# Pre-norm deferred past the input projections of a two-layer encoder trunk

## The chip, the cores and the metric

The kernel runs on one core of a Trainium2 chip. The metric is the device time of one execution in microseconds (us); less is better. The core has five engines that run side by side: PE (TensorE, matrix products and transposes), ACT (ScalarE), DVE (VectorE), POOL (GpSimd) and SP (SyncE, which here only issues DMAs). They meet at semaphores.

## The reference, cut to what matters

Two layers over x (256 tokens, 1024 features). Each layer:

```python
h = _rmsnorm(x, pre_norm_g[i])                 # x / rms(x) * g
z = h @ w_in[i]                                # 1024 -> nine column groups
qa, ka, va, qi, ki, wi, ga, qb, kb, vb, gb = _split_in(z)
# rotary embedding on qa, ka, qi, ki, qb, kb; wi * IDX_HEADS ** -0.5
oa = _dsa_attention(qa, ka, va, qi, ki, wi, top_k)    # indexer picks 64 keys, softmax over these
ob = _diff_attention(qb, kb, vb, lam, lam_init, subln_g[i])
y = concat([oa * silu(ga), ob * silu(gb)]) @ w_out[i]
x = x + _rmsnorm(y, post_norm_g[i])
e = (p[i] @ w_ple_proj[i]) * sigmoid(x @ w_ple_gate[i])
x = x + _rmsnorm(e, ple_norm_g[i])
```

All is float32. p is (2, 1, 256, 256): one embedding input of 256 features for each layer.

## The kernel before

**Tiles.** The tokens are two blocks b of 128 rows. x lives in `resid`. Weights come in units: each is two slices of 128 input rows by 512 columns (512 KB); the indexer's units, `IDX`, have 324 columns (324 KB). `UNITS` (L48) lists them in the order of use: `PLE` (the product with p, one unit for each half n of the output), nine groups of `w_in` (`IDX`, `QB`, `KB`, `VB`, `QA`, `KA`, `VA`, `GB`, `GA`) of four units each, then `WO` and `WG`. SP loads a unit into one of 5 slots of `raw`, and waits first for `lo_done`, that the unit five earlier has been split (L400).

**Split products.** float32 operands are split in two parts, as `w_hi` + `w_lo` (ACT copies, L522; DVE subtracts, L708), and each product is made of three: hi·hi (L951), hi·lo (L952), lo·hi (L953). The activations are transposed by PE (step `t8`, L993: four 128x128 transposes to a half of 512 columns in a PSUM bank `sc`), and are split in the same way (`act_hi` L522, `act_lo` L744).

**Steps.** All engines walk through one list, `layer_steps`, each taking its share of each step. ACT and DVE also carry the units' splits, put in by `all_steps` (`START` by hand for the first ten, the rest some seven or eight pieces ahead of use). A piece `mm` is one unit for one block b, that is six products. The list fixes the order on each engine, so a step that waits on ACT holds back what stands behind it on ACT.

**The pre-norm.** Step `pre` for block b: ACT squares and sums the rows of `resid` (L527), DVE adds eps (L701), POOL takes the power -0.5 (L470), DVE multiplies `resid` by that and by `g_norm`, the weight copied to all partitions (L739, into `work`). Only then can `t8` of h begin (L975), and after it the first `IDX` piece. The weights come by a broadcast load of 512 KB for each layer (L407, L512).

**Around it at the start.** SP issues p, PLE unit 0, x of block 0, PLE unit 1, the pre-norm weight, x of block 1, and the first IDX unit. PE runs warm-up products, transposes p, runs warm-up products again (L970), then the four PLE pieces with the transposes of h between them. POOL issues, after h is made, the next layer's p (L433), the post-norm weight (L506), four small broadcast loads of the lambda vectors (L437) and one of `subln_g` (L438), and the weight `g_ple` (L509).

**At the border of the layers** the last WG pieces of layer 0 are followed by PLE pieces with the transposes of h for block 0, then `IDX` and `QB` for block 0, and the same for block 1.

**Banks.** Four PSUM banks `proj` take the products in turn (`bank_of`, L317; `wait_bank`, L889). ACT evicts them, with plain copies for most groups, sigmoid for the gates.

Of the kernel before, what the change touches and what calls it, by code (L numbers as in the profile page):

```python
# [22 lines left out]
P = 128  # L23
# [24 lines left out]
UNITS = [("PLE", n, 0, KU, N) for n in range(2)]  # L48
# [10 lines left out]
for _i, _u in enumerate(UNITS):  # L59
# [7 lines left out]
START = [1, 2, 5, 8, 11, 11, 16, 17, 18, 19]  # L67
HOLD = 2
# [6 lines left out]
    TI=0,  # L75
    D=3,
    lam=4,
    QB=[4, 5],
    KB=[10, 13],
    QA=[25, 30],  # L80
    KA=[33, 38],
    S=[12, 16, 19, 36, 41, 43],
    E=[12, 18, 23, 37, 41, 44],
    R=[16, 16, 19, 22, 24, 24, 38, 41, 43, 44, 44, 44],
    PT=[19, 23, 26, 41, 42, 44, 46, 49, 50],
    PV=[20, 25, 28, 42, 44, 46, 49, 51, 51],
    hv=[21, 28],
    hn=[23, 30],
    topk=[[0, 0, 1, 4, 6, 6, 8, 12], [12, 24, 24, 26, 26, 27, 31, 31]],
    y=[51, 54])  # L90


def layer_steps(L):
# [26 lines left out]
    ple = [(n, b) for n in range(2) for b in range(NB)]  # L120
    t8 = lambda src, b: [("t8", src, b, 0), ("t8", src, b, 1)]
    y8 = lambda b, half: [("t8", "y", b, half)]
    if L == 0:
        out += [("pT", 0), ("pre", 0, 0)]
        mms("PLE", ple, {0: [("pre", 1, 0)], 2: t8("h", 0), 3: t8("h", 1)})
        mms("IDX", both, {})
        mms("QB", both, {3: [("TI", 0)], 5: [("D", 0)]})
    else:
        out += [("ple0", 1, 1, L - 1)]
        mms("PLE", ple, {0: t8("h", 0) + [("psq", 1, 1, L - 1), ("ple1", 1, L - 1)], 2: [("pre", 1, L)]})  # L130
        mms("IDX", one(0), {})
        mms("QB", one(0), {1: t8("h", 1)})
        mms("IDX", one(1), {})
        mms("QB", one(1), {1: [("TI", 0)], 3: [("D", 0)]})

    mid = [[] for _ in range(7 * len(both))]
    placed = [(PLACE["TI"], ("TI", 1)), (PLACE["D"], ("D", 1)), (PLACE["lam"], ("lam",))]
    for kind in ("S", "E", "R", "PT", "PV"):
        placed += [(i, (kind, n)) for n, i in enumerate(PLACE[kind])]
    for kind in ("hv", "hn"):  # L140
        placed += [(i, (kind, b)) for b, i in enumerate(PLACE[kind])]
# [9 lines left out]
    for c, chunk in enumerate(["KB", "VB", "QA", "KA", "VA", "GB"]):  # L151
        mms(chunk, both, dict(enumerate(mid[c * len(both):(c + 1) * len(both)])))
    mms("GA", one(0) + one(1), dict(enumerate(mid[6 * len(both):])))
# [7 lines left out]
                      12: ([("pre", 0, L + 1)] if L + 1 < DEPTH else []) + [("psq", 1, 0, L)]})  # L161
# [5 lines left out]
def all_steps():  # L167
# [9 lines left out]
    for i, pos in enumerate(pieces):  # L177
# [3 lines left out]
        if L and u < 2 and i - first_use[L * U] < HOLD:  # L181
            held.add(i)
# [5 lines left out]
    at = 0  # L188
# [15 lines left out]
def build(nc, x, p, pre_norm_g, w_in, w_out, post_norm_g, lambda_q1, lambda_k1, lambda_q2, lambda_k2, subln_g,  # L204
# [6 lines left out]
    with ctx:  # L211
# [40 lines left out]
        g_norm = sb("g_norm", [P, D_MODEL])  # L252
        g_ple = sb("g_ple", [P, D_MODEL])
# [35 lines left out]
        x_in = [sem(f"x_in{b}") for b in range(NB)]  # L289
        p_in = [sem(f"p_in{L}") for L in range(DEPTH)]  # L290
        gpre_in = [sem(f"gpre_in{L}") for L in range(DEPTH)]
# [5 lines left out]
        h_done, x1_done, x2_done = sem("h_done"), sem("x1_done"), sem("x2_done")  # L297
# [19 lines left out]
        def bank_of(chunk, n, b):  # L317

            if chunk == "PLE":
                return 2 * (1 - n) + b  # L320
            if chunk in ("WO", "WG"):
                return (2 if b == 0 else 0) + n
            return 2 * (IN_CHUNKS.index(chunk) % 2) + b
# [59 lines left out]
        def _(sp):  # L383
            def load_x(b):
                sp.dma_start(resid[:, b, :], x[0, b * P:(b + 1) * P, :]).then_inc(x_in[b], 16)

            sp.dma_start(p_raw[:, :, :], p[0, 0].rearrange("(b p) d -> p b d", p=P)).then_inc(p_in[0], 16)
            for g in range(DEPTH * U):
                L, u = divmod(g, U)
                chunk, n, k0, nk, cols = UNITS[u]  # L390
                if chunk == "PLE":
                    src = w_ple_proj[L, :, n * N:(n + 1) * N]
# [495 lines left out]
        def _(pe):  # L888
# [39 lines left out]
            for pos, (L, s) in enumerate(STEPS):  # L928
                kind = s[0]
                if kind == "mm":  # L930
# [25 lines left out]
                    elif last_k:  # L956
                        last.then_inc(b0_done, 1)
# [167 lines left out]
```

## Time and profile before

| | |
|---|---|
| median of three runs | 375.98 us (375.42 to 376.27) |
| profiled execution, its own time | 376.63 us |
| its span, first to last instruction | 374.8 us |
| PE busy | 362.0 us (97%) |
| DVE busy | 261.2 us (70%) |
| ACT busy | 223.0 us (59%) |
| POOL busy | 66.7 us (18%) |
| moved from HBM | 60.2 MB |

The busy share of PE counts products from start to modelled end, and they overlap; whether PE is held up is read from the starts of its rows in the timeline. In the timeline a row is an instruction or a run of like ones (x8), with its start, its time, and in brackets what the engine had waited for before it.

### The profile page before, as it was taken

Reading aid. Unit: us, or ns where it says so; the run is one execution under the profiler, and the core shown is the slowest. Engines: PE = TensorE matmul, PEld = TensorE weight load, DVE = VectorE, ACT = ScalarE, POOL = GpSimd, SP = SyncE. Lnnn points to the kernel's source line nnn. Section 1 sums busy time; section 2 is a strip of 40 time slices with the busy share of each in tenths; the row PEclk is TensorE's granted clock in tenths of the full one; section 3 lists DMA queues with packets and bytes.
Section 4 is the critical chain, followed back from the end, with each engine's and each line's share of the span. In section 5 each row is a group of like instructions: output and inputs, shape, how many; then the busy total and the mean of one; then the engine's idle time right before and its main releaser. Section 6 shows DMA issues by size and latency. Waiting matters only on the chain.

```text
span 374.8 us, 5604 instructions
## 1 busy us (share of the span) xinstructions
PE 362.0 (97%) x1932; PEld 300.6 (80%) x1932; DVE 261.2 (70%) x450; ACT 223.0 (59%) x451; POOL 66.7 (18%) x122
## 2 busy tenths in 40 slices
PE   7798999999999999999999999999999999999992
PEld 7596788788877888888889878788887788888881
DVE  2654977889873676587697478788986467558643
ACT  4655674775875753554684548577586575366221
POOL 1514513032500000004005512104150000000000
PEclk9899999999999999999999999999999999999999
DMA  7998846465564354567754845546457335551011
GB/s 251 319 183 312 290 141 186 114 174 162 165 194 149 113 170 143 184 201 146 201 164 150 267 126 157 168 120 207 124 168 226 112 114 168 171 176 47 2 41 71
DMA packets 32075, 61.64 MB, mean 164 GB/s; under 512 B 2384, under 2 KB 4688, under 8 KB 32048
## 3 DMA queue, kind: packets, MB, share of 16 engines
q1 hardware_dynamic: 30928, 58.01, 49.8%
q0 software_dynamic: 1120, 3.28, 4.6%
q8 instruction: 16, 0.26, 0.3%
q14 instruction: 11, 0.09, 0.1%
HBM read 60.23 MB, written 1.05 MB: 163 GB/s over the span
## 4 chain that ended last, share of the span: by engine, by line
PE 88%; DMA 6%; issue 2%; DVE 2%; ACT 1%; SPq 0%; DVEq 0%; POOLq 0%; POOL 0%
PE proj L951 25%; PE proj L953 24%; PE proj L952 23%; PE pv L1091 4%; DMA raw<-in_w_in_dram 3%; PE sc L1063 3%; PE sc L993 3%; DMA g_norm<-in_pre_norm_g_dram 2%; PE tr L1076 2%; PE tr L1009 2%; PE sc L1047 1%; PE sc L1023 1%; DVE w_lo L708 1%; DVE work L739 0%; ACT w_hi L522 0%
## 5 line engine op out<-in xcount | busy, mean ns | idle before, releaser
L951 PE MATMUL proj<-w_hi,act_hi 128*128 128x512 f32 (+1 forms) x416 | 166.4, 400 | 1.3 <-DVE w_lo L708 1.1
L953 PE MATMUL proj<-w_hi,act_lo 128*128 128x512 f32 (+1 forms) x416 | 160.1, 385 | 0.0
L952 PE MATMUL proj<-w_lo,act_hi 128*128 128x512 f32 (+1 forms) x416 | 159.9, 384 | 0.0
L708 DVE TENSOR_TENSOR w_lo<-raw,w_hi 128x1024 fp32r<-128x1024 f32 (+1 forms) x108 | 128.0, 1203 | 17.7 <-ACT w_hi L522 16.9
L522 ACT ACTIVATE w_hi<-raw 128x1024 fp32r<-128x1024 f32 (+1 forms) x108 | 109.9, 1041 | 6.9 <-DMA raw<-in_w_in_dram 4.9
L951 PEld LDWEIGHTS proj<-w_hi,act_hi 128*128 128x128 f32 x416 | 78.2, 188 | 17.3 <-DVE w_lo L708 1.3
L953 PEld LDWEIGHTS proj<-w_hi,act_lo 128*128 128x128 f32 x416 | 78.1, 188 | 16.0
L952 PEld LDWEIGHTS proj<-w_lo,act_hi 128*128 128x128 f32 x416 | 78.3, 188 | 12.8
L470 POOL TENSOR_TENSOR rstd<-var,minus_half 128x1 f32<-128x1 f32 x12 | 6.7, 554 | 192.2 <-DVE var L698 177.0
L625 ACT ACTIVATE probs<-sc,neg_max 128x128 f32<-128x128 f32 (+1 forms) x64 | 26.0, 429 | 13.4 <-DVE neg_max L796 13.4
L522 ACT ACTIVATE act_hi<-sc 128x512 fp32r<-128x512 f32 x24 | 13.6, 597 | 32.7 <-PE sc L993 32.7
L796 DVE TENSOR_REDUCE neg_max<-sc 128x2 f32<-128x512 f32 (+1 forms) x24 | 15.5, 686 | 17.5 <-PE sc L1063 17.5
L744 DVE TENSOR_TENSOR act_lo<-sc,act_hi 128x512 fp32r<-128x512 f32 x24 | 15.9, 686 | 15.2 <-ACT act_hi L522 15.0
L522 ACT ACTIVATE pT<-tr 128x512 f32<-128x512 f32 (+1 forms) x22 | 12.7, 578 | 22.3 <-PE tr L1076 20.3
L1091 PEld LDWEIGHTS pv<-v_all,pT 128*128 128x128 f32 x144 | 18.5, 191 | 1.3
L1091 PE MATMUL pv<-v_all,pT 128*128 128x64 f32 (+1 forms) x144 | 18.1, 271 | 0.0
L460 POOL TENSOR_TENSOR v_all<-work,rot_tab 128x128 f32<-128x128 f32 x16 | 12.1, 756 | 32.4 <-ACT work L522 31.4
L492 POOL TENSOR_TENSOR rstd_h<-var_h,minus_half 128x4 f32<-128x4 f32 x4 | 4.1, 1032 | 58.0 <-DVE var_h L838 58.0
L625 ACT ACTIVATION_READ_ACCUMULATOR probs<-sc,neg_max 128x1 f32 x64 | 13.8, 215 | 0.0
L522 ACT ACTIVATE work<-proj 128x512 f32<-128x512 f32 x16 | 9.6, 597 | 5.5 <-PE proj L953 5.5
L872 DVE TENSOR_TENSOR work<-work,emb 128x512 f32<-128x512 f32 x8 | 5.5, 686 | 10.2 <-ACT work L658 10.2
L785 DVE MAX8 top<-score 128x8 f32<-128x128 f32 (+1 forms) x32 | 11.4, 356 | 0.6
(124 smaller groups left out, 368.6 us busy)
## 6 DMA issues: line engine op xcount, KB each, us to landing
raw<-in_w_in_dram SPq DMA_DIRECT2D x64, 512.0 KB, 4.1
raw<-in_w_out_dram SPq DMA_DIRECT2D x16, 512.0 KB, 3.4
raw<-in_w_ple_gate_dram SPq DMA_DIRECT2D x16, 512.0 KB, 4.1
raw<-in_w_in_dram SPq DMA_DIRECT2D x8, 324.0 KB, 7.2
raw<-in_w_ple_proj_dram SPq DMA_DIRECT2D x4, 512.0 KB, 3.4
resid<-in_x_dram SPq DMA_DIRECT2D x2, 512.0 KB, 7.5
g_norm<-in_post_norm_g_dram POOLq DMA_DIRECT2D x2, 512.0 KB, 5.6
g_ple<-in_ple_norm_g_dram POOLq DMA_DIRECT2D x2, 512.0 KB, 7.5
```

Source lines behind the costliest of these rows:

```text
L460: nc.gpsimd.tensor_tensor(rot_a[:, 0:heads, :], view[:, :, 0:ROT], table(cos2, slice(0, ROT)), ALU.mult)
L522: return nc.scalar.activation(dst, src, ACT.Copy, scale=scale)
L625: last = nc.scalar.activation(probs[:, i % 4, j * keys:(j + 1) * keys], sc[i % 2][:, j * keys:(j + 1) * keys], ACT.Exp, bias=neg_max[:, i ...
L708: nc.vector.tensor_tensor(w_lo[:, g % SLOTS, 0:nk * cols], raw[:, g % RAW_SLOTS, 0:nk * cols], w_hi[:, g % SLOTS, 0:nk * cols].bitcast(fp3 ...
L744: nc.vector.tensor_tensor(act_lo[:, s[2], 4 * s[3]:4 * s[3] + 4, :].rearrange("p k t -> p (k t)"), sc[i % 2][:, :], act_hi[:, s[2], 4 * s[ ...
L785: link(nc.vector.max(top8[:, :], score[b][:, :]))
L796: nc.vector.tensor_reduce(neg_max[:, i % 2, 0:len(maps)], sc[i % 2][:, :].rearrange("p (m k) -> p m k", k=keys), AX.X, ALU.max, negate=Tru ...
L951: nc.tensor.matmul(ps, src_hi[:, b, k0 + k, :], hi, start=(first_u and k == 0), stop=False)
L952: nc.tensor.matmul(ps, src_hi[:, b, k0 + k, :], lo, start=False, stop=False)
L953: last = nc.tensor.matmul(ps, src_lo[:, b, k0 + k, :], hi, start=False, stop=last_k)
L993: last = nc.tensor.transpose(sc[i % 2][:, j * P:(j + 1) * P], tile, ident[:, :])
L1091: last = nc.tensor.matmul(pv[:, h * width:(h + 1) * width], pT[:, n % 3, j, :], v_all[:, kt, g, h * width:(h + 1) * width], start=(kt == 0 ...
```

## The change

It has five parts.

1. The pre-norm is taken apart. `t8` of h now transposes x itself, as soon as it is there (block and half by themselves). The weight of the pre-norm, which after the transpose lies along partitions, is applied on eviction: ACT copies four 128x128 pieces with a scale from a column of `g_col`, DVE subtracts with the same scale. 1/rms of a token is applied to the projections: on each ACT eviction (scale by `rstd`), and for the gates in the sigmoid's scale and in DVE's product. The factor `IDX_HEADS ** -0.5` moves into the relu's scale. The multiplication of `resid` into `work` is gone.
2. `g_col` is made once: a load of 8 KB with the weights of both layers, one transpose on PE (step `gT`), one copy on ACT. The two broadcast loads of 512 KB are gone.
3. PLE units are one slice each (256 KB, three products a piece), four in place of two. x comes in four loads of 256 KB, behind the PLE units.
4. The order: in both layers eight PLE pieces, then `IDX` for block 0, `IDX` for block 1, then `QB` and the rest. `pre` (the sum of squares) stands behind the transposes. `PLACE` and `START` are rewritten for it.
5. `bank_of` depends on the layer, and IDX takes the banks of PLE half 0. The small loads, and the next layer's p, are issued right after p is transposed; the post-norm weight and `g_ple` of layer 0 only at the third PV step.

```diff
-UNITS = [("PLE", n, 0, KU, N) for n in range(2)]
+UNITS = [("PLE", n, k, 1, N) for n in range(2) for k in range(D_PLE // P)]
...
-START = [1, 2, 5, 8, 11, 11, 16, 17, 18, 19]
-HOLD = 2
...
+    h00=[5, 5],
+    h01=[8, 8],
+    pre0=[9, 11],
+    psq=1,
+    ple1=3,
+    h10=[0, 3],
+    h11=[8, 10],
+    pre1=[10, 12],
+    HOLD=0,
+    START=[1, 1, 3, 3, 8, 11, 12, 12, 17, 18])
...
     if L == 0:
-        out += [("pT", 0), ("pre", 0, 0)]
-        mms("PLE", ple, {0: [("pre", 1, 0)], 2: t8("h", 0), 3: t8("h", 1)})
-        mms("IDX", both, {})
-        mms("QB", both, {3: [("TI", 0)], 5: [("D", 0)]})
+        out += [("pT", 0), ("gT",)]
+        side = []
...
+    side += [(i, ("t8", "h", b, half)) for b in range(NB) for half, i in enumerate(PLACE[f"h{L}{b}"])]
+    side += [(i, ("pre", b, L)) for b, i in enumerate(PLACE[f"pre{L}"])]
+    head = ple + [(len(ple) // NB + u, b) for u, b in one(0) + one(1)]
+    mms("PLE", head, {i: [step for at, step in side if at == i] for i in range(len(head))})
...
+                bank = 2 * ((IN_CHUNKS.index(chunk) + 1) % 2) + b
+            return bank ^ 2 * (L % 2)
...
                 if g == 0:
-                    load_x(0)
-                elif g == 1:
-                    sp.dma_start(g_norm[:, :], pre_norm_g[0, :].partition_broadcast(P)).then_inc(gpre_in[0], 16)
-                    load_x(1)
-                elif g == 2:
+                    sp.dma_start(g_rows[:, :], pre_norm_g.rearrange("l (k p) -> (l k) p", p=P)).then_inc(gpre_in, 16)
+                elif g == 3:
+                    load_x(0, 0)
+                    load_x(0, 1)
+                elif g == 4:
+                    load_x(1, 0)
+                    load_x(1, 1)
+                elif g == 5:
...
-                if kind == "t8" and s[1:] == ("h", 1, 1):
-                    pool.wait_ge(h_done, L * 2 + 2)
+                if kind == "pT" and s[1] + 1 < DEPTH:
+                    pool.wait_ge(ptr_done, s[1] + 1)
+                    load_p(s[1] + 1)
+                if kind == "pT" and s[1] == 0:
+                    load_small(0)
+                if kind == "PV" and s[1] == 2:
+                    if L > 0:
+                        pool.wait_ge(wo_scaled, L * 4)
                     pool.dma_start(g_norm[:, :], bcast(post_norm_g[L, :])).then_inc(gpost_in, 16)
                     if L == 0:
-                        load_small(0)
                         pool.dma_start(g_ple[:, :], bcast(ple_norm_g[0, :])).then_inc(gple_in, 16)
...
-                        copy(z_idx[:, b, 0:nqk], ps[:, 0:nqk])
+                        act.wait_ge(rstd_done[0], L * 2 + b + 1)
+                        copy(z_idx[:, b, 0:nqk], ps[:, 0:nqk], rstd[:, 0, b:b + 1])
...
-                        copy(z_view(chunk, b), ps[:, :]).then_inc(z_out, 1)
+                        copy(z_view(chunk, b), ps[:, :], rstd[:, 0, b:b + 1]).then_inc(z_out, 1)
...
+                    if s[1] == "h":
+                        act.wait_ge(gcol_done, 1)
+                        for j in range(4):
+                            k = 4 * s[3] + j
+                            last = copy(act_hi[:, s[2], k, :], sc[i % 2][:, j * P:(j + 1) * P],
+                                        g_col[:, L * KT + k:L * KT + k + 1])
+                        last.then_inc(at_hi, 1)
+                        continue
...
-                    nc.vector.tensor_tensor(gate[:, b, :], proj[bank_of(chunk, n, b)][:, :], gate[:, b, :], ALU.mult)\
+                    nc.vector.scalar_tensor_tensor(gate[:, b, :], proj[bank_of(L, chunk, n, b)][:, :],
+                                                   rstd[:, 0, b:b + 1], gate[:, b, :], ALU.mult, ALU.mult)\
...
                     add_eps(0, M, b, 1)
-                    dve.wait_ge(rstd_done[0], M * 2 + b + 1)
-                    dve.wait_ge(gpre_in[M], 16)
-                    nc.vector.scalar_tensor_tensor(work[:, b, :], resid[:, b, :], rstd[:, 0, b:b + 1], g_norm[:, :],
-                                                   ALU.mult, ALU.mult).then_inc(h_done, 1)
...
+                    if s[1] == "h":
+                        for j in range(4):
+                            k = 4 * s[3] + j
+                            ins = nc.vector.scalar_tensor_tensor(
+                                act_lo[:, s[2], k, :], sc[i % 2][:, j * P:(j + 1) * P],
+                                g_col[:, L * KT + k:L * KT + k + 1], act_hi[:, s[2], k, :].bitcast(fp32), ALU.mult,
+                                ALU.subtract)
+                        ins.then_inc(at_lo, 1)
+                        continue
```

## Rows read from the trace of the kernel before

**Rows 1.** The page: PE's busy share in 40 slices of the span, in tenths.

```profile
PE   7798999999999999999999999999999999999992
```

**Rows 2.** Waits of PE over the whole span: us, times, longest.

```profile
PE proj L951 <- DVE w_lo L708: 3.4, 2, 2.3
```

**Rows 3.** Stretches: length, busy time by engine, clock share, DMA share, GB/s.

```profile
16.40:18.50 2.10, 2.10 (x8) 1.72 (x8) 1.71 (x3) 1.42 (x3) 2.10 (x5) 0.58 0.92 248
34.10:60.00 25.90, 25.83 (x127) 20.59 (x128) 21.48 (x46) 17.03 (x27) 12.68 (x20) 1.00 0.67 209
```

**Rows 4.** Timeline of the start, PE, with the DVE row in its gap.

```profile
8.05 0.48 PE L951 MATMUL proj<-w_hi,p_hi 128*128 128x512 f32 x1
...
10.64 0.39 PE L953 MATMUL proj<-w_hi,p_lo 128*128 128x512 f32 x1
10.87 1.28 DVE L739 SCALAR_TENSOR_TENSOR work<-resid,rstd,g_norm 128x1024 f32<-128x1024 f32 x1 [1.57 <-DMA g_norm<-in_pre_norm_g_dram]
...
13.34 0.50 PE L951 MATMUL proj<-w_hi,p_hi 128*128 128x512 f32 x1 [2.31 <-DVE w_lo L708]
...
14.90 1.91 PE L993 MATMUL sc<-ident,work 128*128 128x128 f32 x8
...
16.46 0.78 PE L951 MATMUL proj<-w_hi,p_hi 128*128 128x512 f32 x1
...
18.25 0.40 PE L952 MATMUL proj<-w_lo,p_hi 128*128 128x512 f32 x1
...
18.71 1.04 PE L993 MATMUL sc<-ident,work 128*128 128x128 f32 x8
...
20.87 0.39 PE L951 MATMUL proj<-w_hi,act_hi 128*128 128x324 f32 x1 [0.23 <-DVE act_lo L744]
```

**Rows 5.** Timeline of the start: ACT rows released by the two loads of x.

```profile
7.95 1.06 ACT L527 ACTIVATE work<-resid 128x1024 f32<-128x1024 f32 x1 [1.25 <-DMA resid<-in_x_dram]
...
12.08 1.06 ACT L527 ACTIVATE work<-resid 128x1024 f32<-128x1024 f32 x1 [1.27 <-DMA resid<-in_x_dram]
```

**Rows 6.** Timeline: first QB product, and the second gap of PE.

```profile
27.16 0.39 PE L951 MATMUL proj<-w_hi,act_hi 128*128 128x512 f32 x1
...
31.80 1.06 ACT L522 ACTIVATE w_hi<-raw 128x1024 fp32r<-128x1024 f32 x1 [4.71 <-DMA raw<-in_w_in_dram]
...
32.60 0.49 PE L1000 MATMUL tr<-ident,v_all 128*128 128x128 f32 x3
...
34.17 0.50 PE L951 MATMUL proj<-w_hi,act_hi 128*128 128x512 f32 x1 [1.08 <-DVE w_lo L708]
```

**Rows 7.** Stretches of the DMA, columns as in rows 3.

```profile
22.00:24.00 2.00, 2.00 (x15) 2.00 (x15) 2.00 (x4) 1.64 (x2) 0.00 (x0) 1.00 1.19 42
24.00:26.00 2.00, 2.00 (x16) 2.00 (x15) 1.09 (x1) 0.00 (x0) 0.00 (x0) 1.00 0.57 57
...
30.00:32.00 2.00, 2.00 (x11) 1.65 (x10) 0.00 (x0) 0.20 (x1) 0.00 (x0) 1.00 1.03 393
...
178.00:180.00 2.00, 2.00 (x10) 1.65 (x9) 0.88 (x2) 1.77 (x4) 0.00 (x0) 1.00 0.66 22
```

**Rows 8.** Timeline of POOL: the small loads at the start.

```profile
16.25 1.08 POOL L437 DMA_DIRECT2D lam_in<-in_lambda_q_dram  x2
```

**Rows 9.** Groups by line and shape: busy us, mean ns, idle before.

```profile
L744 DVE TENSOR_TENSOR act_lo<-sc,act_hi 128x512 fp32r<-128x512 f32 x24 | 15.9, 686 | 15.2 <-ACT act_hi L522 15.0
...
L522 ACT ACTIVATE act_hi<-sc 128x512 fp32r<-128x512 f32 x24 | 13.6, 597 | 32.7 <-PE sc L993 32.7
...
L642 ACT ACTIVATE qT_b<-pv,row_rec 128x128 f32<-128x128 f32 x16 | 5.7, 368 | 8.1 <-PE pv L1091 8.1
...
L847 DVE SCALAR_TENSOR_TENSOR qT_b<-pv,scale_h,g_sub 128x128 f32<-128x128 f32 x16 | 4.5, 344 | 0.1
```

**Rows 10.** Timeline at the layers' border: ACT evicts the last gate, DVE ends layer 0.

```profile
191.38 0.60 ACT L658 ACTIVATE work<-proj 128x512 f32<-128x512 f32 x1
...
198.37 1.41 DVE L883 SCALAR_TENSOR_TENSOR resid<-qT_a,rstd,resid 128x512 f32<-128x512 f32 x2 [0.66 <-POOL rstd L470]
```

More of the change, by code:

```diff
@@ L119, in layer_steps @@
     one = lambda b, n=UQ: [(u, b) for u in range(n)]
-    ple = [(n, b) for n in range(2) for b in range(NB)]
+    ple = [(u, b) for u in range(FIRST["IDX"]) for b in range(NB)]
     t8 = lambda src, b: [("t8", src, b, 0), ("t8", src, b, 1)]
@@ L123, in layer_steps @@
     if L == 0:
-        out += [("pT", 0), ("pre", 0, 0)]
-        mms("PLE", ple, {0: [("pre", 1, 0)], 2: t8("h", 0), 3: t8("h", 1)})
-        mms("IDX", both, {})
-        mms("QB", both, {3: [("TI", 0)], 5: [("D", 0)]})
+        out += [("pT", 0), ("gT",)]
+        side = []
     else:
         out += [("ple0", 1, 1, L - 1)]
[L130 to L137, printed above, removed]
+        side = [(PLACE["psq"], ("psq", 1, 1, L - 1)), (PLACE["ple1"], ("ple1", 1, L - 1))]
+    side += [(i, ("t8", "h", b, half)) for b in range(NB) for half, i in enumerate(PLACE[f"h{L}{b}"])]
+    side += [(i, ("pre", b, L)) for b, i in enumerate(PLACE[f"pre{L}"])]
+    head = ple + [(len(ple) // NB + u, b) for u, b in one(0) + one(1)]
+    mms("PLE", head, {i: [step for at, step in side if at == i] for i in range(len(head))})
+    mid = [[] for _ in range(8 * len(both))]
+    placed = [(PLACE["lam"], ("lam",))]
     for kind in ("S", "E", "R", "PT", "PV"):
         placed += [(i, (kind, n)) for n, i in enumerate(PLACE[kind])]
-    for kind in ("hv", "hn"):
+    for kind in ("TI", "D", "hv", "hn"):
         placed += [(i, (kind, b)) for b, i in enumerate(PLACE[kind])]
@@ L150, in layer_steps @@
         mid[i].append(step)
-    for c, chunk in enumerate(["KB", "VB", "QA", "KA", "VA", "GB"]):
+    for c, chunk in enumerate(["QB", "KB", "VB", "QA", "KA", "VA", "GB"]):
         mms(chunk, both, dict(enumerate(mid[c * len(both):(c + 1) * len(both)])))
-    mms("GA", one(0) + one(1), dict(enumerate(mid[6 * len(both):])))
+    mms("GA", one(0) + one(1), dict(enumerate(mid[7 * len(both):])))
     mixed = [(u, 0) for u in (0, 1, 2, 3, 4)] + [(u, 1) for u in (0, 1)] + [(u, 0) for u in (5, 6, 7)] \
@@ L160, in layer_steps @@
                       10: [("ple0", 0, 1, L), ("psq", 0, 1, L)], 11: [("ple1", 0, L), ("ple0", 1, 0, L)],
-                      12: ([("pre", 0, L + 1)] if L + 1 < DEPTH else []) + [("psq", 1, 0, L)]})
+                      12: [("psq", 1, 0, L)]})
     if L + 1 == DEPTH:
@@ L180, in all_steps @@
         last_use[L * U + u] = i
-        if L and u < 2 and i - first_use[L * U] < HOLD:
+        if L and i - first_use[L * U] < PLACE["HOLD"]:
             held.add(i)
@@ L568, in _ @@
                                 act.wait_ge(y_done, (L - 1) * 4 + 2 + b + 1)
-                        nc.scalar.activation(gate[:, b, :], ps[:, :], ACT.Sigmoid).then_inc(sig_done, 1)
+                        nc.scalar.activation(gate[:, b, :], ps[:, :], ACT.Sigmoid, scale=rstd[:, 0, b:b + 1])\
+                            .then_inc(sig_done, 1)
+                elif kind == "gT":
+                    act.wait_ge(gcol_tr, 1)
+                    copy(g_col[:, :], tr[:, 0:DEPTH * KT]).then_inc(gcol_done, 1)
                 elif kind == "pT":
@@ L577, in _ @@
                     if M == 0:
-                        act.wait_ge(x_in[b], 16)
+                        for half in range(2):
+                            act.wait_ge(x_in[b][half], 16)
                     else:
@@ L973, in _ @@
                     i = t8_index(src, b, half)
-                    if src == "h":
-                        pe.wait_ge(h_done, L * 2 + b + 1)
+                    if src == "h" and L == 0:
+                        pe.wait_ge(x_in[b][half], 16)
+                    elif src == "h":
+                        pe.wait_ge(x2_done, (L - 1) * 4 + 2 * b + half + 1)
                     elif src == "y":
```

98 lines of the change are left out of this document (50 added, 48 removed).

## The prediction

> **What bounds the kernel now.** I read the page first: PE's busy share is 9 in every slice but the first two, the third and the last [rows 1], so from about 30 us on the time is PE's. Then the waits of PE: only 3.4 us on the weights' split in the whole span, in two waits [rows 2]. The stretches say the same: from 34.1 to 60 us PE is busy 25.83 of 25.90 us at full clock, with DVE at 21.5 and ACT at 17.0 [rows 3]. An edit past 34 us can therefore lose time but hardly win any, unless it takes products away, and this one takes none: PLE's 24 products a layer stay 24, the 32 transposes of h stay 32, and one small transpose comes. What can be won lies ahead of 34.17 us, and I list it from the starts of PE's rows.
>
> (a) The products of the first two PLE pieces start 0.23 us apart, from 8.05 to 10.64; the next starts at 13.34 [rows 4]. That is 2.70 us where 0.23 was due: 2.47 us lost. It waited for the split of PLE unit 1, which on DVE stood behind the multiplication of x (L739, 10.87 to 12.15), which had itself waited 1.57 us for the broadcast weight [rows 4].
>
> (b) After that gap the clock falls: 0.58 of full in 16.4 to 18.5 us [rows 3], which is the lower level, 1.2 GHz, for most of it. The first eight transposes take 1.91 us, the next eight, at 2.4 GHz again, 1.04: 0.87 us lost. The four products from 16.46 to 18.25 take 1.79 us where four times 0.23 is 0.92: another 0.87 [rows 4]. Together 1.7 us.
>
> (c) 0.23 us of waiting for `act_lo` at 20.87 [rows 4].
>
> (d) The three transposes at 32.60 are followed by a product only at 34.17: 1.57 us, of which three transposes need 0.33, at some 0.11 each (an estimate: eight take 1.04 with the last one's end [rows 4]): 1.24 lost. Its unit had landed at 31.80, after ACT had waited 4.7 us [rows 6]. The DMA had been close to standing still: 42 and 57 GB/s in 22 to 26 us, against 393 in 30 to 32 [rows 7]. POOL had issued the small lambda loads from 16.25 on [rows 8]; nothing else was new on the queues, so I put the standstill down to them. In layer 1 the same loads go with 22 GB/s in 178 to 180 us [rows 7], there without any wait of PE.
>
> Total to be won: 2.47 + 1.7 + 0.2 + 1.24 = 5.6 us. The first product at 8.05 stays: warm-up products fill PE until then, and they are not changed.
>
> **The change part by part.** *Front of the start.* Transposes no longer wait for squares, root, weight and multiplication. PE runs PLE at once: step `gT` adds one transpose, 0.11 to 0.2 us (its 8 KB load is third in the queue, and PE is in its warm-up until 8.05). Splits of 512 columns cost about half of a unit's; ACT does units 2 and 3 after `gT`, from 8.4 us on, DVE has the third by about 10.0 and PE needs it at 8.2 + 12 x 0.23 = 10.9. So (a) goes, and with no gap there I let (b) go too.
>
> *Loads.* Between the landing of x block 0 at 7.95 and of x block 1 at 12.08 three loads of 512 KB land [rows 5], so 0.69 us for 256 KB. By 7.95 the queue had moved p, PLE 0 and x 0, 1280 KB; now that is p and the four PLE units. Then x block 0 at 9.3, the first IDX unit (324 KB) at 10.2, x block 1 at 11.6; the next layer's p (256 KB), now issued at about 5.2 on POOL's queue, adds 0.7 to these at most. The second IDX unit waits for the split of unit 0 (about 7.2 us), the fourth for that of unit 2 (about 10.0): landings some 13.2, 14.1, 15.0. PE wants x block 0 at 12.3 and block 1 at about 16.2: margins of 2.3 us and more. Each load of 256 KB costs SP another issue of 0.5 us, hidden, since one takes less than its 0.69 us of transfer.
>
> *The path through ACT and DVE gets longer.* Where one copy of 128x512 took 597 ns and one subtraction 686 [rows 9], there are now four of 128x128. The nearest rows with a scale from a column are ACT's L642 at 368 ns and DVE's L847 at 344 [rows 9]. Run without overlap four are 1.5 and 1.4 us; ACT at 597 and DVE at 686 for the same elements is the other end. Instructions in a row overlap a little, so I take 1.2 each: 2.4 us and a start-up of 0.3 in place of 1.3 and 0.3. Then, with PLE as 24 products and two times eight transposes: six PLE pieces end at 8.2 + 18 x 0.23 = 12.3; block 0's transposes 0.87; last PLE unit to 14.5. The first half of h is split by 12.75 + 2.7 = 15.3, so the first IDX piece waits 0.8 us (0 to 1.2 by the ends). DVE's row continues: second half of h 16.4, IDX unit 1 at 17.3, unit 2 at 18.6; PE asks at 17.0 and 18.2: 0.3 and 0.4. Block 1's first half is split after units 2 and 3 are, behind in the order, at 20.8, PE asks at 20.4: 0.4. New waits 1.9 us, spread over 6 us and none as long as the one that went with the clock's fall (0 to 3 us by the ends).
>
> A page's price for the same: the Trainium skill (ScalarE: Activation LUTs, "What ACT_TABLE_LOAD costs") gives a fixed part for each ACTIVATE, some 93 ns more for each operand that is a column, and an overlap of about as much between neighbours. The row of 368 ns for 128x128 with a column [rows 9] agrees with it; four pieces would be 1.27 us by the page where I took 1.2, and the sum would move by 0.1 us.
>
> *(d).* The small loads are now issued from about 6.1 to 8.8 us. The unit that was late at 31.80 had been queued behind them; the QB units will now be behind nothing. (d) goes. What the standstill does at its new place is the first rival.
>
> *Behind 34 us.* ACT gets 24 more copies for h (8 halves at about +0.6, 5 us), a column operand on some 26 evictions (2.5 us), DVE 24 more subtractions (+4 us) less four multiplications of 1.28 (5.1 us). Both have idle time in every stretch, ACT 9 of 26 us, DVE 4 [rows 3]: cover enough, cost 0; if the cover is gone it is at most the 2 us by which ACT's load rises ahead of the softmax pieces. The post-norm weight and `g_ple` go to the third PV step, 1 MB behind about 85 us on POOL's queue, while the DMA is near 0.6 busy; needed at the WO stage some 60 us later; hidden. The eviction of IDX now waits for 1/rms: `pre` stands two pieces ahead of it, and behind the wait on ACT are two splits with seven pieces (4.8 us) of lead; price 0 to 0.9. At the border, x of block 1 is complete 8.4 us after the last gate is evicted (191.38 to 199.8 [rows 10]); now PE asks for it after 24 PLE products, eight transposes and an IDX piece, 7.2 us after that gate; but `ple1` loses the splits of h between, and stands behind fewer large units. I take 0, with 0 to 1.2 us as bounds. Banks: IDX takes the pair that PLE half 0 left four pieces earlier. 0.
>
> *Sum.* 5.6 - 0.15 (gT) - 1.9 (new waits) = 3.55 us won. Against the profiled execution: span 374.8 to 371.2, its own time 376.63 to 373.1. The median of the runs lies 0.65 below that execution: 375.98 to 372.4.
>
> **The rivals.**
> A. The standstill of the small loads hits the start. It moved 50 GB/s where 390 were to be had, for 4 us at the start and some 3 in layer 1: 2.6 to 3.5 us of transfer lost. For it: they are now issued at 6.1 us, in the middle of the loads that PE waits for. Against it: margins of 2 us. It costs 3 less 2, about 1 us, for the units of IDX, up to 3 if it comes before x is through. Gain 0.5 to 3: 373.0 to 375.5.
> B. The new waits don't show (the four pieces overlap well, and DVE is less behind than I lay out): 5.6 - 0.15 = 5.4, time 370.5 to 371.8.
> C. Slower: the same standstill, but before the first IDX unit has landed. Then PE stands at 14.5 us until about 18.6, 4.1 us in a row, longer than the 2.3 us [rows 4] after which the clock fell; it falls again, 1.7 us. 5.6 - 0.15 - 1.1 (the later waits) - 4.1 - 1.7 = -1.5, and with the second IDX unit as late again -2.5: 377.3 to 378.5. It decides from the point where that unit lands past about 16 us. Against: by my count its packets are through before 10 us, and in both cases seen the standstill came 2 us or so after the small loads' own start.
> D. The change moves the wait only: ACT stands at the IDX eviction for 1/rms, and x is now behind four PLE loads. What is gained before 14 us is given back by 27.16 us, the first QB product [rows 6], and (d) is all that stays or not even that: 375.3 to 376.5. Against: 1/rms is off PE's path until the banks come round.
>
> **How the numbers follow.** My forecast 0.46 (371.8 to 373.0), A 0.26, B 0.12, C 0.09, D 0.07. The predicted time is 372.4 us. The range takes B's lower end, 370.4, and A to its upper end, 375.4; C and D stay out, 0.16. A measurement of this kernel can tell some 0.2% from none, 0.75 us: faster means under 375.2. Faster 0.46 + 0.12 + nearly all of A = 0.83; within 0.2%: D and a little of A, 0.08; slower 0.09.
>
> **What would show it.** In the profile after: no gap of PE between PLE pieces; clock share 1.00 from 10 to 20 us; first transposes of x at about 12.3; small waits of PE on `act_lo` and `w_lo` between 14 and 21 us, together about 1.9; first QB product at about 24.5 in place of 27.16; no wait at the transposes of the indexer; from there PE packed as before, every step some 3.6 us earlier. Stretches of 8 to 16 us under 100 GB/s would speak for A or C, a wait of PE of over 2 us on a split of IDX with a fallen clock for C. ACT idle for long before the first IDX copy, with PE waiting behind it, for D. The prediction is wrong if PE is held up in the border stretch, or if an order set by `PLACE` makes it wait on a step in the middle.

## The result and the profile after

The changed kernel takes 379.64 us (median of 4 runs, 379.4 to 379.71) against 375.70 us for the kernel before in the same comparison. The ratio is 1.0113, with a 95% interval of 1.0091 to 1.0135: slower by 1.1%, where 372.4 us were forecast. The profiled execution has a span of 377.9 us (before 374.8) and a mean clock of 0.988 (before 0.993).

First the waits of PE over the whole span, the same view as rows 2 (who waited for whom, us in total, times, longest). One line more stands ahead of these in it, a wait of 2.2 us for POOL at the very start, which the kernel before has too:

```profile
PE proj L987 <- DVE w_lo L738: 2.0, 1, 2.0
PE sc L1033 <- DMA resid<-in_x_dram: 1.7, 1, 1.7
PE proj L987 <- DVE act_lo L774: 1.4, 1, 1.4
```

Three waits, 5.1 us in all, where the kernel before had 3.6. A wait of about 2 us on `w_lo` it had too (2.3 us, [rows 4]); new are one straight on a load of x, and one of 1.4 us on `act_lo` where it was 0.2. The timeline of the start shows them in place; it answers to rows 4 and 5:

```profile
12.15 1.03 PE L1033 MATMUL sc<-ident,resid 128*128 128x128 f32 x8
12.88 0.74 ACT L536 ACTIVATE w_hi<-raw 128x648 fp32r<-128x648 f32 x1 [1.30 <-DMA raw<-in_w_in_dram]
...
15.96 0.39 PE L987 MATMUL proj<-w_hi,act_hi 128*128 128x324 f32 x1 [1.41 <-DVE act_lo L774]
...
16.93 0.60 PE L1033 MATMUL sc<-ident,resid 128*128 128x128 f32 x4
19.21 0.65 PE L1033 MATMUL sc<-ident,resid 128*128 128x128 f32 x4 [1.68 <-DMA resid<-in_x_dram]
20.16 0.74 ACT L536 ACTIVATE w_hi<-raw 128x648 fp32r<-128x648 f32 x1 [3.98 <-DMA raw<-in_w_in_dram]
21.82 0.64 PE L987 MATMUL proj<-w_hi,act_hi 128*128 128x324 f32 x1 [1.96 <-DVE w_lo L738]
22.26 0.47 PE L988 MATMUL proj<-w_lo,act_hi 128*128 128x324 f32 x1
```

Until 14.4 us PE goes as forecast: the transposes of block 0 start at 12.15 (forecast 12.3), and there is no gap between the PLE pieces. The loads do not: the first IDX unit is there at 12.88 where 10.2 was forecast, and the chain behind it on ACT starts late. Then the second half of block 1 of x lands at 19.2 us, the second IDX unit at 20.16, and PE does eight transposes and one piece between 14.4 and 21.8 us. The stretches tell where the loads were (length, busy time by engine with counts, clock share, DMA share, GB/s):

```profile
10.00:12.00 2.00, 2.00 (x11) 1.64 (x10) 0.74 (x2) 1.22 (x3) 0.00 (x0) 1.00 1.11 357
12.00:14.00 2.00, 2.00 (x15) 1.74 (x14) 0.34 (x1) 1.12 (x3) 0.00 (x0) 1.00 1.06 99
14.00:16.00 2.00, 0.59 (x4) 0.20 (x2) 1.80 (x7) 2.00 (x8) 0.00 (x0) 1.00 0.94 130
16.00:18.00 2.00, 1.53 (x10) 1.29 (x10) 0.85 (x4) 0.18 (x1) 0.00 (x0) 1.00 0.85 191
18.00:20.00 2.00, 0.65 (x4) 0.42 (x4) 0.00 (x0) 0.00 (x0) 0.00 (x0) 1.00 0.92 326
20.00:27.00 7.00, 5.18 (x19) 5.18 (x20) 4.79 (x13) 6.84 (x16) 0.57 (x1) 0.54 0.85 301
```

From 12 to 18 us the DMA engines are busy (shares 0.85 to 1.06) and deliver 99 to 191 GB/s: the pattern of rows 7, now in the middle of the start. And in 20 to 27 us the clock share is 0.54: after waits of 1.4 and 1.7 us, and inside the third, of 2.0, the granted clock falls to the lower level, 1.2 GHz, and the IDX products come 0.27 us apart instead of 0.15.

The starts of four of PE's rows place the 3.1 us (us from the span's start; each is the first product of its kind):

| | before | after | change of the step to it |
|---|---|---|---|
| first PLE product | 8.05 | 7.89 | -0.16 |
| first QB product | 27.16 | 30.64 | +3.64 |
| first PLE product of layer 1 | 191.18 | 193.57 | -1.09 |
| last product | 367.42 | 370.49 | +0.69 |

So the start loses 3.6 us where by the forecast's sum it was to win 2.3 (5.6 less 1.24 for the wait of rows 6, 0.15 and 1.9). The wait of rows 6 is gone as forecast, but the stretch that held it gets only 1.09 us shorter, and layer 1 loses another 0.7 where nothing was forecast.

### The profile page after: what moved, and what is told of

Its sections match the earlier page's. It is cut to its first block, busy times and chain, and to the rows that moved or that the text cites. A ratio compares the mean times of both kernels' runs of the same rounds, so it can differ in the third digit from the quotient of the medians.

```text
span 377.9 us, 5688 instructions
## 1 busy us (share of the span) xinstructions
PE 363.6 (96%) x1933; PEld 301.8 (80%) x1933; DVE 260.1 (69%) x474; ACT 231.4 (61%) x480; POOL 70.2 (19%) x121
## 4 chain that ended last, share of the span: by engine, by line
PE 91%; DMA 3%; issue 2%; DVE 1%; ACT 1%; POOL 0%; DVEq 0%; POOLq 0%
PE proj L987 26%; PE proj L989 24%; PE proj L988 24%; PE pv L1131 4%; DMA raw<-in_w_in_dram 3%; PE sc L1103 3%; PE sc L1033 2%; PE tr L1116 2%; PE tr L1049 2%; PE sc L1087 1%; PE sc L1063 1%; PE pv L963 1%; DVE w_lo L738 0%; PE tr L1040 0%; PE pv L1006 0%
## 5 line engine op out<-in xcount | busy, mean ns | idle before, releaser
L738 DVE TENSOR_TENSOR w_lo<-raw,w_hi 128x1024 fp32r<-128x1024 f32 (+2 forms) x112 | 129.3, 1166 | 20.3 <-ACT w_hi L536 19.4
L536 ACT ACTIVATE w_hi<-raw 128x1024 fp32r<-128x1024 f32 (+2 forms) x112 | 111.1, 1014 | 8.5 <-DMA raw<-in_w_in_dram 5.3
L988 PEld LDWEIGHTS proj<-w_lo,act_hi 128*128 128x128 f32 x416 | 79.4, 191 | 12.9
L484 POOL TENSOR_TENSOR rstd<-var,minus_half 128x1 f32<-128x1 f32 x12 | 8.5, 708 | 196.3 <-DVE var L728 173.6
L536 ACT ACTIVATE act_hi<-sc 128x512 fp32r<-128x512 f32 x16 | 9.2, 598 | 28.9 <-PE sc L1033 28.9
L474 POOL TENSOR_TENSOR v_all<-work,rot_tab 128x128 f32<-128x128 f32 x16 | 14.0, 873 | 32.5 <-ACT work L536 31.4
L780 DVE TENSOR_TENSOR act_lo<-sc,act_hi 128x512 fp32r<-128x512 f32 x16 | 10.7, 687 | 13.4 <-ACT act_hi L536 13.4
L536 ACT ACTIVATE work<-proj,rstd 128x512 f32<-128x512 f32 x16 | 11.0, 689 | 5.1 <-PE proj L989 5.0
L688 ACT ACTIVATE work<-proj 128x512 f32<-128x512 f32 x8 | 4.8, 600 | 13.1 <-PE proj L989 13.1
```

The costliest lines, as they stand in the source:

```text
L474: nc.gpsimd.tensor_tensor(rot_a[:, 0:heads, :], view[:, :, 0:ROT], table(cos2, slice(0, ROT)), ALU.mult)
L484: nc.gpsimd.tensor_tensor(rstd[:, i, b:b + 1], var[:, i, b:b + 1], minus_half[:, 0:1], ALU.pow).then_inc(rstd_done[i], 1)
L536: return nc.scalar.activation(dst, src, ACT.Copy, scale=scale)
L738: nc.vector.tensor_tensor(w_lo[:, g % SLOTS, 0:nk * cols], raw[:, g % RAW_SLOTS, 0:nk * cols], w_hi[:, g % SLOTS, 0:nk * cols].bitcast(fp3 ...
L780: nc.vector.tensor_tensor(act_lo[:, s[2], 4 * s[3]:4 * s[3] + 4, :].rearrange("p k t -> p (k t)"), sc[i % 2][:, :], act_hi[:, s[2], 4 * s[ ...
L988: nc.tensor.matmul(ps, src_hi[:, b, k0 + k, :], lo, start=False, stop=False)
```

## The experiments

The theory from here: the small broadcast loads of layer 0, issued at 6.4 us instead of 16.3, slow the DMA while x and the first weights are on their way (theory 1). The rival: the longer path through ACT and DVE, and x behind four PLE loads, hold PE up by themselves (theory 2). The runs come from three comparisons, with the kernel before beside them at a median of 375.13, 375.34 and 375.45 us; between kernels of two comparisons, differences under half a microsecond say little.

### The small loads to one partition

The loads stay where they are, but move 1/128 of the bytes. POOL also fills the other partitions with constants, by two memsets at the very start.

```diff
+                rows = 1 if L == 0 else P
                 for i, v in enumerate((lambda_q1, lambda_q2, lambda_k1, lambda_k2)):
-                    pool.dma_start(lam_in[:, i, :], bcast(v[L, :])).then_inc(small_in, 16)
+                    pool.dma_start(lam_in[0:rows, i, :], v[L, :].partition_broadcast(rows)).then_inc(small_in, 16)
...
```

> The changed kernel with one thing taken away: in layer 0 the four lambda vectors and the sub-norm weight are loaded to one partition instead of to all 128 (the other partitions hold constants, so layer 0's lambda and sub-norm weight are not the reference's). Theory 1, the standstill of the small broadcast loads delays block 1 of x and the second IDX unit: both land by about 12 and 14 us, PE's waits of 1.7 us on x and 2.0 us on the split are gone, and the clock does not fall in 20 to 27 us; time 372 to 374 us. Theory 2, the four-piece evictions and x behind the PLE loads are the cause: PE still waits for over 1.5 us in two places between 14 and 22 us, time 377 us or more.

Measured: 373.3 us; ratio to the kernel before 0.9947 (0.9927 to 0.9968). Of PE's waits behind the warm-up only 0.7 us on `act_lo` stay; first QB product at 24.39. Theory 1 holds, and theory 2 is out as the cause of the loss. The five loads together, 192 KB of some 60 MB, cost 6.3 us.

### The small loads late

All of them, full size, but issued after the second sum of squares; this kernel computes everything.

```diff
-                if kind == "pT" and s[1] == 0:
-                    load_small(0)
...
                 elif kind == "pre":
                     inv_sqrt(0, s[2], s[1])
+                    if L == 0 and s[1] == 1:
+                        load_small(0)
```

> The changed kernel with the small broadcast loads of layer 0 issued after the second sum of squares (about 22 us) instead of after p is transposed. Theory 1: the start as in the run with one-row loads, first QB product at 25 to 27 us; the standstill now falls among the QB and KB units and may cost up to 1.5 us there as it did in the kernel before; time 372.5 to 375.5 us. Theory 2: 377 us or more.

Measured: 372.61 us (372.41 to 373.01); ratio 0.9935 (0.9913 to 0.9957). It is faster than both kernels: by 2.5 us than the kernel before (375.13 us beside it), by 7.0 than the changed one, and what parts it from the changed one is the place of five loads. The stretches of this run:

```profile
12.00:14.00 2.00, 2.00 (x14) 1.65 (x12) 1.12 (x3) 1.53 (x7) 0.00 (x0) 1.00 1.10 344
14.00:16.00 2.00, 1.33 (x10) 1.11 (x9) 2.00 (x8) 2.00 (x6) 0.00 (x0) 1.00 1.06 382
16.00:18.00 2.00, 2.00 (x16) 1.77 (x15) 1.72 (x3) 2.00 (x6) 0.00 (x0) 1.00 0.91 259
...
28.00:30.00 2.00, 2.00 (x11) 1.64 (x10) 1.95 (x2) 2.00 (x3) 1.98 (x3) 1.00 0.75 49
```

The loads now run at 259 to 382 GB/s in the start, the standstill comes at 28 to 30 us (49 GB/s), and PE is busy for the whole of that stretch: the weights are far enough ahead by then. How long the four loads of x were under way is told by their line, in the changed kernel and then in this one (issue to landing, us, min/median/max):

```profile
DMA to landing us min/median/max: 6.5/9.1/13.4
```

```profile
DMA to landing us min/median/max: 5.3/6.2/6.9
```

The slowest of them loses 6.5 us.

### The next layer's p late

```diff
-                if kind == "pT" and s[1] + 1 < DEPTH:
-                    pool.wait_ge(ptr_done, s[1] + 1)
-                    load_p(s[1] + 1)
                 if kind == "pT" and s[1] == 0:
+                    pool.wait_ge(ptr_done, 1)
                     load_small(0)
                 if kind == "PV" and s[1] == 2:
+                    if L + 1 < DEPTH:
+                        pool.wait_ge(ptr_done, L + 1)
+                        load_p(L + 1)
```

> The changed kernel with the next layer's p (256 KB) loaded at the third PV step instead of in the start; the small loads stay early. If the bytes of p matter (0.7 us of transfer), x of block 1 lands 0.7 us earlier and the time falls by 0.5 to 1 us to about 379. If only the small loads matter, they start sooner and the standstill merely comes earlier: 379 to 381 us.

Measured: 377.92 us (376.54 to 379.01, 6 runs), 1.7 us less than the changed kernel: more than the 0.5 to 1 expected from the bytes, and the standstill stays (109 GB/s in 12 to 14 us, and one wait of PE of 3.0 us on `w_lo`). Neither of the two expectations had this number. The first IDX unit was through ahead of the standstill (its split starts at 11.95 instead of 12.88), and the clock was down for 3.4 us instead of 6.8. How much a standstill costs depends, by these two runs, on which load it catches.

### The kernel before with the small loads early

```diff
+                if kind == "pT" and s[1] == 0:
+                    pool.wait_ge(ptr_done, 1)
+                    load_small(0)
...
-                        load_small(0)
```

> The kernel before with one thing changed: the small broadcast loads of layer 0 are issued right after p is transposed (about 5.5 us), as in the changed kernel. Theory 1: the loads of x block 1 and of the IDX units come 3 us or more later, PE stands and the clock falls for longer; part of it comes back as the wait at 34 us goes; time 377 to 380 us, slower than before by 1 to 4. Theory 2: no change beyond 0.5 us, or faster by 1.2 as the wait at 34 us goes.

Measured: 378.6 us; ratio 1.0109 (1.0063 to 1.0155). One moved call makes the kernel before as slow as the changed one. Its timeline:

```profile
15.08 1.06 ACT L529 ACTIVATE work<-resid 128x1024 f32<-128x1024 f32 x1 [4.68 <-DMA resid<-in_x_dram]
...
18.19 0.74 ACT L524 ACTIVATE w_hi<-raw 128x648 fp32r<-128x648 f32 x1 [1.48 <-DMA raw<-in_w_in_dram]
20.77 1.60 PE L995 MATMUL sc<-ident,work 128*128 128x128 f32 x8 [4.22 <-DVE act_lo L746]
```

Block 1 of x is there at 15.08 instead of 12.08 [rows 5], PE stands for 4.2 us in one piece, and the clock falls after it (0.50 in 22 to 24 us). Nothing of the deferred norm is in this kernel, so theory 2 has no part in the loss.

### Why these loads are slow: each partition its own row

Same place, same shapes, same bytes, but the source has a row for each partition.

```diff
-                    pool.dma_start(lam_in[:, i, :], bcast(v[L, :])).then_inc(small_in, 16)
+                    src = bcast(v[L, :]) if L else w_out[0, 0:P, i * HEAD:(i + 1) * HEAD]
+                    pool.dma_start(lam_in[:, i, :], src).then_inc(small_in, 16)
...
```

> The changed kernel, the small loads early as in it and of the same shapes and bytes, but in layer 0 each partition reads its own row of another tensor instead of all 128 reading one row (so layer 0's lambda and sub-norm weight are not the reference's). If reading one address from all partitions is what makes the packets slow, the standstill in 10 to 18 us is gone: 372.5 to 374.5 us. If short rows of 256 and 512 bytes are slow by themselves, it stays: 378.5 us or more.

Measured: 372.52 us; ratio 0.9921 (0.9901 to 0.994). The same stretches:

```profile
12.00:14.00 2.00, 1.83 (x10) 1.21 (x8) 1.12 (x5) 1.97 (x8) 0.00 (x0) 1.00 1.09 311
14.00:16.00 2.00, 1.52 (x12) 1.54 (x13) 2.00 (x7) 2.00 (x5) 0.00 (x0) 1.00 1.07 369
16.00:18.00 2.00, 2.00 (x15) 1.77 (x14) 1.71 (x3) 2.00 (x6) 0.00 (x0) 1.00 1.05 382
```

No standstill. The queue of the loads that POOL issues shows the same in its own account of 0 to 40 us (packets, MB, share of the time of 16 engines), first in the changed kernel, then in this one:

```profile
q0 software_dynamic: 240, 0.46, 10.7%
```

```profile
q0 software_dynamic: 240, 0.46, 3.2%
```

The same number of packets and the same bytes, but 68 us of the engines' time against 20, or 4.3 and 1.3 us on each of the 16. In the trace's packet records the four lambda loads are 64 packets of 2 KB, eight rows each: they took 344 ns in the median and up to 1.87 us in the changed kernel, 87 and at most 148 ns here. Rows of 256 and 512 bytes are not slow by themselves; 128 reads of one such row are. (The run reads another tensor as well as other addresses, and no run reads 128 rows of a small tensor, so the part of the tensor itself was not tested.) The Trainium skill (DMA: Bandwidth & Descriptors, "Specifications") puts the smallest transfer for full rate at 512 bytes, which would have blamed the rows of 256; here such rows at their own addresses cost nothing that the stretches show, so the measurement goes against it as an explanation. Why repeated reads of one short row are slow, while the 512 KB broadcast of the pre-norm weight (4 KB rows) went along in the kernel before without such a stretch, no run here settles.

### The kernel before without the small loads, and with them later

> The kernel before with the small loads of layer 0 to one partition each (layer 0's lambda and sub-norm weight are not the reference's). If the standstill is what made the QB unit late at 31.80 us, the 1.24 us before 34.17 go: about 374 us, 1.2 less than before, which leaves only some 1.3 us for the rest of the change. If the unit was late for another reason: no change.

The edit is that of the first experiment. Measured: 373.36 us (10 runs); ratio 0.996 (0.994 to 0.998). That is 2.0 us less than the kernel before beside it, where 1.2 were expected; the 0.8 us more are taken up below. The wait before 34 us is gone: from the first QB product to the first PLE product of layer 1 it takes 162.60 us instead of 164.02.

> The kernel before with nothing changed but the place of layer 0's small broadcast loads: issued behind the first rotary step of IDX (about 28 us) instead of at 16 us. If the standstill is harmless once weights are ahead, as in layer 1 and in the changed kernel with late loads, it runs as the one-row variant of the kernel before: 373 to 374 us, and the deferred norm by itself is worth only what then separates it from 372.6, some 0.7 us. If the QB and KB units are not far enough ahead at 30 to 35 us, a wait of about 1 us stays: 374.5 to 375.5 us.

```diff
                         rope_rows(z_idx[:, b, :].rearrange("p (h d) -> p h d", d=HEAD), 6, b, rope_idx,
                                   L * 2 + b + 1)
+                        if L == 0 and b == 0:
+                            load_small(0)
```

Measured: 373.73 us (12 runs); ratio 0.9952 (0.9929 to 0.9975). The standstill sits at 34 to 36 us, behind the place where it hurt:

```profile
34.00:36.00 2.00, 2.00 (x11) 1.58 (x9) 0.91 (x1) 1.06 (x2) 0.94 (x4) 1.00 0.76 60
```

PE loses nothing to it. So of the 2.5 to 2.8 us that the changed kernels with late small loads are ahead of the kernel before, 1.7 to 2 are to be had by moving one call, and 0.5 to 1.1 are left for the deferred norm and the new order.

The 22 runs of these two kernels fall in two groups, and the groups part by the mean clock of the run: 14 runs at 372.6 to 374.0 us (median 373.0) with a clock of 0.993 or more, 8 at 374.9 to 375.7 (median 375.2) with 0.989 or 0.990. The profiled execution of the one is of the first group, that of the other of the second. Their gap of PE, and the stretch behind it (14 to 19 us), first one row, then late:

```profile
13.21 0.50 PE L955 MATMUL proj<-w_hi,p_hi 128*128 128x512 f32 x1 [2.18 <-DVE w_lo L712]
...
14.00:19.00 5.00, 5.00 (x32) 4.11 (x30) 4.65 (x7) 4.39 (x9) 4.25 (x9) 1.00 0.89 259
```

```profile
PE proj L952 <- DVE w_lo L709: 2.6, 1, 2.6
...
14.00:19.00 5.00, 5.00 (x20) 4.21 (x21) 3.68 (x5) 3.27 (x6) 2.52 (x4) 0.66 0.78 241
```

After gaps of 2.2 and 2.6 us the clock stays in one run and falls in the other. Only these two executions are seen in a profile; that the other 20 part in the same way is read from their mean clock alone, and this is a rough mark (the profiled execution of the kernel before has 0.993 with a fall). With that said, the fall of (b) in the prediction is not a fixed 1.7 us but a cost of about 2 us that some of the runs pay. The four runs of the changed kernel with late small loads have a mean clock of 0.997 each, and lie within 0.6 us; against the 14 runs at 373.0 (from the other two comparisons) they are ahead by only 0.4.

In the kernel before itself, of its 40 runs beside these experiments, the 18 with a clock of 0.989 or 0.990 have a median of 375.5 us and the 17 with 0.995 or more one of 375.1: there the clock is worth 0.4 us or less, not 2. This fits with the late QB unit. It lands when the standstill lets it, whether PE was fast before or not, so what PE gains by a clock that stays up it gives back in the wait at 34 us. The two losses (b) and (d) then lie one behind the other in the profiled run, but are not independent of each other. That reading is argued from the times; no profile of the kernel before shows a clock that stayed up.

### The price of the four pieces

Late small loads, and the pre-norm weight left out, so that h is evicted whole.

```diff
                     if s[1] == "h":
                         act.wait_ge(gcol_done, 1)
+                    if False:
                         for j in range(4):
...
-                    if s[1] == "h":
+                    if False:
                         for j in range(4):
```

> The kernel with the late small loads, and the pre-norm weight left out: h is evicted by one copy and one subtraction of 128x512 as before, instead of four and four. This prices the pieces. By the sum of the prediction they cost up to 1.9 us of new waits, of which the late run showed 0.83 before the first IDX piece and about 0.4 behind it: with whole evictions 371.2 to 371.9 us. If the waits have another cause, no change from 372.6.

Measured: 371.55 us; ratio 0.9889 (0.9872 to 0.9906). By the two medians the pieces cost 1.06 us, by the two ratios to the kernel before (0.9889 and 0.9935) 1.7; the profile has 1.2 in the start, so about 1.1 to 1.7. PE has no wait on `act_lo` or `w_lo` left, and the first QB product comes 14.68 us after the first PLE product instead of 15.86.

### One half of the transposes earlier, and the halves together in layer 1

```diff
-    h00=[5, 5],
+    h00=[4, 5],
...
-    START=[1, 1, 3, 3, 8, 11, 12, 12, 17, 18])
+    START=[1, 1, 3, 3, 7, 11, 12, 12, 17, 18])
```

> The kernel with the late small loads; the first half of block 0's transposes stands one PLE piece earlier (after the fifth piece instead of the sixth), and the first IDX unit's split with it. If the first IDX piece waits only for the chain transpose, four copies, four subtractions, then 0.68 us of its 0.83 us wait go: 371.9 us. If x had not landed by then, the wait moves to the transposes: 372.6 us.

Measured: 372.5 us against 372.61, both with 4 runs: no difference that this measurement can tell. In the profile the wait of 0.83 us is down to 0.13, and first PLE to first QB product takes 15.30 us instead of 15.86. But the first PLE product itself came at 8.07 instead of 7.61, as the 16 warm-up products from 4.92 us on took 3.06 us instead of 2.60; over all profiles here it lies between 7.13 and 8.61 us, which hides half a microsecond. What makes it move is not shown by the granted clock, which is 1.00 there in both.

> The reordered kernel with the late small loads; in layer 1 the two halves of each block's transposes stand together (two places instead of four). The changed kernel takes some 0.8 us more than the kernel before from the first QB product to the last product. If that is the return from transposes to products, at about 0.1 to 0.15 us each, two of them go: 0.2 to 0.3 us less from first QB to last product, time 372.1 to 372.4 us. If it is something else in layer 1, no change from 372.5.

The edit sets `h10=[0, 0]` and `h11=[9, 9]` as well. Measured: 372.77 us (6 runs). Expected were 0.2 to 0.3 us less, found were none: layer 1 takes 177.0 us from its first PLE product to the last product, against 176.8 with the halves apart. Two returns from transposes are gone, and waits are there, the first row in layer 0, the second in layer 1:

```profile
15.24 0.39 PE L987 MATMUL proj<-w_hi,act_hi 128*128 128x324 f32 x1 [1.14 <-DVE act_lo L774]
...
197.85 0.39 PE L987 MATMUL proj<-w_hi,act_hi 128*128 128x324 f32 x1 [0.26 <-DVE act_lo L774]
```

The first of these rows shows also why the earlier half did not always pay: the chain before it starts with a split that waited for its load,

```profile
12.16 0.74 ACT L536 ACTIVATE w_hi<-raw 128x648 fp32r<-128x648 f32 x1 [1.07 <-DMA raw<-in_w_in_dram]
```

so that in this run the transposed half lay ready while ACT, in order, stood at the first IDX unit.

## Why the prediction was wrong, point by point

**What bounds the kernel, and (a).** Right: no gap between PLE pieces, block 0's transposes at 12.15.

**(d).** Right in cause and about in size: without the small loads or with them elsewhere, the kernel before gets 1.4 us faster between first QB product and layer 1, where 1.24 were forecast. In the sum it stands beside (b) as if the two were independent, which the runs by clock group speak against.

**The step that failed: the standstill against the margins.** The prediction saw the small loads go to 6.1 us, named their standstill as the first rival, and priced it there: 3 us of transfer lost, less margins of 2 us, about 1 us. In the forecast's own sum it stands at nothing. The runs put it at 6.3 to 7.0 us (changed kernel against one row and against late). The amount of transfer was right. Between 12 and 18 us the changed kernel moved 249, 250 and 86 GB/s less than the one-row run (348, 380 and 277 GB/s in the three stretches), 1.17 MB, or 3.1 us at 380 GB/s. Wrong was to set that against a margin as if it delayed every load by its share: the four loads of x took up to 13.4 us in place of 6.9. Counted by bytes, the queue of x and the weights had moved at 17.0 us in the changed kernel what it had moved at 12.6 in the late run, when the last load of x was there; that load landed at 19.2. So 4.4 of its 6.5 us are bytes that came later, and 2 us it lay behind even that. That slow packets of the small loads stood in the way of single parts of it would fit, but no run shows it by itself. A margin has to be held against the slowest load, and no row of the kernel before was used for that, though one was at hand: the unit that landed at 31.80 [rows 6] had been issued at 19.0, and the view of L401 for 18 to 19.5 us says of it

```profile
DMA to landing us min/median/max: 12.8/12.8/12.8
```

The count of the loads themselves was nearly right: with the 0.7 us allowed for p it had block 1 of x at 12.3 us and the first IDX unit at 10.9, and in the late run they are there at 12.6 and by 11.16. What was not laid beside it is when the standstill comes. In the kernel before it was 5.75 us from the first issue (16.25 [rows 8]) to the stretch at 42 GB/s (from 22.00 on [rows 7]). The same distance from 6.1 gives about 12 us, with block 1 of x just landing and the second IDX unit still to come; the changed kernel shows 99 GB/s from 12.0 on.

**The clock.** Of the rivals only C had it, after one gap of 4.1 us; the run had waits of 1.4, 1.7 and 2.0 us, and the clock share at 0.54 for seven us. The excess of the IDX products there is about 2.5 us, so of the 6.9 us more from first PLE to first QB product (22.75 against 15.86 in the late run) some 4.4 are waits (5.05 against 0.67). C was put at 377.3 to 378.5 with a chance of 0.09, and its condition, a landing of the first IDX unit past 16 us, was not met (12.88); it was block 1 of x and the second unit, which the prediction had given margins of 2 us and more. Sign and mechanism were C's, place and weight were not.

**The longer path.** Forecast 1.9 us of new waits, 0 to 3. The late run shows 0.83 ahead of the first IDX piece and about 0.3 behind it, and leaving the pieces out gives 1.1 to 1.7. The four copies with a column run 2.16 us for eight, that is about 1.1 a half (1.2 was taken). The price was right for the first wait; the later ones did not add up. That each wait of PE gives the engines behind it time to catch up would explain it, but was not tested.

**Behind 34 us: cost 0.** Wrong by 0.8 us in the late run and by 1.0 in the changed kernel. In layer 0, from the first QB product to layer 1, they take 162.84 and 162.93 us where the kernel before without its wait takes 162.60. Layer 1, from its first PLE product to the last product, takes 176.80 and 176.92 us instead of 176.24. About 0.1 of it goes when the pieces are left out (176.69). Some 0.3 us are lost in the head of the layer, by its 144th product, where the halves are transposed in four places and the order is new; moving the halves together did not win them back. The rest comes later in the layer. The cause of neither is shown.

**The sum.** With the small loads late the forecast kernel exists: 372.61 us, forecast 372.4. That the two are so near is luck in good part. Of the new waits 0.8 us more were forecast than came, and 0.8 us fewer behind 34 us. And the forecast started from a profiled execution of 376.63 us and took 0.65 off, by three runs; the 40 runs on record of the kernel before, beside the experiments, have medians of 375.1 to 375.5. Against these the late kernel wins 2.5 us, not the 3.6 forecast (ratio 0.9935, 0.9913 to 0.9957, where the forecast is 0.9905). In the profiled executions it wins 4.2 us (376.63 to 372.41). The sum was made from one execution, which took 1.2 to 1.5 us more than these medians.

A small slip stands in the signs: a first QB product at 24.5 is 2.7 us earlier than 27.16, while the terms that lie ahead of it add up to 2.3.

## What to carry to other kernels

When a change moves a load, ask what shares the queues at its new place, and hold the margin of each load that the critical engine needs against the slowest landing the trace shows in such company, not against the mean rate. Small loads that copy one short row to all partitions belong where weights are well ahead; here their place alone was worth 7 us of 380, more than the whole restructuring. Try the placement by itself first: moving one call in the old kernel gave two thirds of what the whole change could. And before adding up losses from one profile, see whether that execution is like the median one.

## What the runs showed of the hardware

128 reads of one row of 256 or 512 bytes hold up the DMA engines: 192 KB asked for in this way cut the rate to 42 to 130 GB/s for some 2 to 6 us, while the same bytes from rows of their own left it at 311 to 382 GB/s. The engines mostly look busy meanwhile (a share of 1.06 at 99 GB/s, 1.19 at 42 [rows 7]), so the DMA's busy share alone does not show it; the GB/s beside it do.

PE's clock stayed up after a gap of 2.2 us in one profiled execution, and fell to 1.2 GHz after gaps of 2.3 and 2.6 us in two others. By the mean clock it fell in 8 of 22 runs of two kernels that have such a gap, and these runs take about 2 us longer; what decides it is not shown. A median over few runs can lie in either group.
